# A two-layer hybrid diffusion backbone: first normalisation stage two tiles ahead, mean pools inside the pool projection, late row stores on ScalarE's queue

## The reference

```
ada = silu(cond) @ w_ada[l] + b_ada[l]            # 6 rows of 1024 per layer: shift, scale, gate, twice
u   = layer_norm(x) * (1 + sc1) + sh1
proj = u @ w_in_even                               # q 512 | k 128 | v 128 | p 512
pool = (mean of p over a window of 2, 4, 8 or 16 tokens) - p, per group of 128 channels
attn = attention(rms_norm(q), rms_norm(k), v)
x = layer_norm(alpha * x + g1 * (concat(attn, mix(pool)) @ w_out))
```

## Time and profile before

| | us |
|---|---|
| median of three executions | 2863.35 |
| the profiled execution | 2858.01 |
| its span | 2856.4 |
| first stage, until the last tile is in `act_a` | 0 to 122 |
| pool projection with the late half-blocks | 122 to 205 |
| q, k, v projection | 209 to 312 |

### The profile page before, as it was taken

The page is one execution under the profiler, slowest core; times in us unless marked ns, Lnnn a source line. Parts: engine busy times, 40 slices in busy tenths (PEclk is TensorE's granted clock), DMA queues, the critical chain, the costliest instruction groups (busy, mean ns, idle before and its releaser), DMA issues.

```text
span 2856.4 us, 36166 instructions
## 1 busy us (share of the span) xinstructions
PE 2682.8 (94%) x13884; PEld 2381.2 (83%) x13884; DVE 1537.1 (54%) x2157; ACT 921.3 (32%) x1402; POOL 432.5 (15%) x258
## 2 busy tenths in 40 slices
PE   5698799999899999999998799999899999999997
PEld 2477577768899999999997799978899999999996
DVE  1316588866555555555557433346555555555557
ACT  2521377745422222222124521125422222222223
POOL 1125277734000000000005200014000000000002
PEclk7899899999999999999999899999999999999999
DMA  9770100022311111111111212122311111111112
GB/s 335 270 262 7 60 1 0 1 90 74 133 45 44 44 44 37 44 30 44 37 45 67 74 45 74 56 92 79 128 45 44 44 44 42 39 39 35 38 35 81
DMA packets 171521, 196.08 MB, mean 69 GB/s; under 512 B 7628, under 2 KB 125880, under 8 KB 171442
## 3 DMA queue, kind: packets, MB, share of 16 engines
q1 hardware_dynamic: 169748, 194.33, 20.6%
q0 software_dynamic: 1280, 0.33, 0.1%
q10 hardware_dynamic: 411, 0.34, 0.0%
HBM read 175.64 MB, written 19.33 MB: 68 GB/s over the span
## 4 chain that ended last, share of the span: by engine, by line
PE 81%; DVE 7%; ACT 5%; POOL 3%; issue 2%; DMA 2%; SPq 0%; ACTq 0%; POOLq 0%; DVEq 0%
PE ps L2011 47%; PE ps L2231 18%; PE ps L1978 5%; POOL p_low L814 2%; PE ps L1961 1%; DVE small L1538 1%; ACT ln_u L939 1%; DVE stats L1391 1%; PE ps L2063 1%; PE ps L2164 1%; ACT p_exp L1068 1%; ACT p_top L870 1%; DMA ada_w<-in_w_ada 1%; PE ps L1923 1%; PE ps L2121 1%
## 5 line engine op out<-in xcount | busy, mean ns | idle before, releaser
L2011 PE MATMUL ps<-act_b,uw 128*128 128x384 f32 x4608 | 807.2, 337 | 7.9 <-DVE act_b L1357 6.5
L2011 PEld LDWEIGHTS ps<-act_b,uw 128*128 128x128 f32 x4608 | 803.5, 189 | 9.8 <-DVE act_b L1357 7.0
L2011 PEld LDWEIGHTS ps<-act_a,uw 128*128 128x128 f32 x3456 | 606.7, 190 | 17.5 <-issue 9.2
L2011 PE MATMUL ps<-act_a,uw 128*128 128x384 f32 x3456 | 613.2, 339 | 6.8 <-DVE act_a L1357 5.3
L2231 PE MATMUL ps<-dw,hh 128*128 128x512 f32 x2112 | 503.8, 398 | 9.0 <-DVE acc L1651 8.8
L2231 PEld LDWEIGHTS ps<-dw,hh 128*128 128x128 f32 x2112 | 398.7, 189 | 109.1 <-DVE acc L1651 10.2
L1651 DVE TENSOR_TENSOR acc<-acc,ps 128x512 f32<-128x512 f32 x360 | 246.0, 687 | 216.0 <-PE ps L2231 216.0
L870 ACT ACTIVATE fa<-ps 128x384 f32<-128x384 f32 (+2 forms) x176 | 67.3, 410 | 838.7 <-PE ps L2011 838.7
L1357 DVE TENSOR_TENSOR uw<-raw_u,uw 128x1024 fp32r<-128x1024 f32 x112 | 136.6, 1221 | 120.6 <-ACT uw L870 117.3
L1612 DVE TENSOR_SCALAR ft<-fa,fgrp 128x1153 f32<-128x1153 f32 x44 | 38.8, 881 | 298.9 <-ACT fa L870 284.1
L814 POOL TENSOR_TENSOR p_low<-p_exp,p_top 128x1536 fp32r<-128x1536 f32 (+1 forms) x50 | 170.6, 3412 | 94.8 <-ACT p_top L870 94.8
(11 more groups left out here) (208 smaller groups left out, 3127.2 us busy)
## 6 DMA issues: line engine op xcount, KB each, us to landing
raw_u<-in_w_up SPq DMA_DIRECT2D x88, 512.0 KB, 4.0
ada_w<-in_w_ada SPq DMA_DIRECT2D x52, 512.0 KB, 6.8
late_w<-in_w_ada SPq DMA_DIRECT2D x44, 512.0 KB, 6.3
raw_d<-in_w_down SPq DMA_DIRECT2D x44, 512.0 KB, 3.7
raw_u<-in_w_in_odd SPq DMA_DIRECT2D x20, 512.0 KB, 3.9
ln_y<-in_x_all SPq DMA_DIRECT2D x18, 512.0 KB, 5.4
xs<-ln_y SPq DMA_DIRECT2D x18, 512.0 KB, 2.6
acc<-xs SPq DMA_DIRECT2D x6, 1536.0 KB, 12.0
```

Of the source, the lines that this page charges most:

```text
L2011: mm = pe.matmul(out, uw[:, u_slot, w, k, :], src[:, k, a, c * CH:(c + 1) * CH], start=(k, w, a) == (0, 0, 0), stop=(k, w, a) == (KD - 1, ...
```

## The change

Cut to its core; what is left out renames or repeats.

```diff
 def ada_half(m):                     # other columns for m = 4 to 13, same set
 def ada_steps(kind):
-    return {s: [4 + s] for s in range(9)} if kind == "in" else {}
+    return {s: [s + 2] for s in range(2, 11)} if kind == "in" else {}
-        ada_row = at("ada_row", [P, 3, 512], F32, off_s + 28672)
+        ada_row = at("ada_row", [P, 6, 512], F32, off_s + 24576)
+        ada_side = at("ada_side", [P, 3, 512], F32, off_s + 12288)
# SP
-                        sp.wait_ge(z_rdy, NT)
+                        sp.wait_ge(zt_done, NT)
-            for m in range(3):
-                ada_units(m)
+            ada_units(0)
+            ada_units(1)
+            first_x(0)
+            ada_units(2)
+            ada_units(3)
+            first_x(1)
+            first_x(2)
+            ada_units(4)
             for n in range(2):
                 u_unit(n, u_source(n))
-            ada_units(3)
-            for s in range(3):
-                sp.dma_start(ln_y[:, s, :], dram_rows(t["x_all"], s)).then_inc(x_ld[s], 16)
-            ada_units(4)
-                            sp.wait_ge(z_rdy, tile + (NT * i4 + 1))
+                            sp.wait_ge(zt_done if i1 is None else z_rdy, tile + (NT * i4 + 1))
-                        for m in ada_steps(kind).get(3 + j, []):
-                            ada_units(m, i)
+                        if i1 is None:
+                            ada_units(5 + j, i)
-            for n in range(2, 4):
-                u_unit(n, u_source(n))
-            for k in range(2):
-                d_unit(D_QKV + k, t["w_in_even"][0][k * P:(k + 1) * P, 0:AW], AW)
             ln_loads("in", t["x_all"])
+            ada_units(11)
+            u_unit(2, u_source(2))
+            u_unit(3, u_source(3))
+            wq_unit(0)
+            wq_unit(1)
+            ada_units(12)
# GpSimd
-            for m in range(ADA_TOP, ADA_ALL):
+            for m in range(ADA_TOP, ADA_LATE):
...
-            gp.wait_ge(bank_free[0], 3 + 6)
-            gp.wait_ge(bank_free[1], 3 + 6)
-            gp.wait_ge(brow_mm, 6)
-            for a in range(2):
-                o = gp.memset(vv[:, :, a, 1, :].bitcast(F32), 1.0 - a)
-            o.then_inc(v_one, 1)
+            gp.wait_ge(u_split, 2 + U_FFN0)
             for g, w in enumerate(WINDOWS):
+                gp.wait_ge(bank_free[g % 2], 3 * (g // 2 + 2))
+                if g == NPG - 1:
+                    gp.wait_ge(brow_mm, 6)
+                    for a in range(2):
+                        o = gp.memset(vv[:, :, a, 1, :].bitcast(F32), 1.0 - a)
+                    o.then_inc(v_one, 1)
# ScalarE
             def late_evac(m):
                 copy(late_row[e % 2][:], ps[:, 6 + m % 2, :]).then_inc(ada_bank, 1)
+                act.wait_ge(ada_bank, m + 4)
+                for c in range(2):
+                    act.dma_start(ada[l, c::2, half * 512:half * 512 + 512], late_row[e % 2][c::32, :]).then_inc(late_st[e % 2], 16)
-            for m in range(ADA_TOP):
+            for m in range(2):
                 top_evac(m)
-            for n in range(2):
-                u_hi_at(n, 0, n)
+            def first_norm(s):
+                if s.live(2):
+                    tile = s.tile(2)
+                    if s.first(2):
+                        act.wait_ge(cols_done, 2)
+                    act.wait_ge(zt_done, tile + 1)
+                    if not s.first(2):
+                        act.wait_ge(act_rdy, tile)
+                    for k in range(KD):
+                        o = act.activation(ln_u[:, k * P:(k + 1) * P], ps[:, 6 + k // 4, (k % 4) * P:(k % 4 + 1) * P], ACT.Identity, ...)
+                    o.then_inc(mod_done, 1)
+                st, y = stats[:, s.slot(0), :], ln_y[:, s.slot(0), :]
+                if s.live(0):
+                    act.wait_ge(stat2, s.tile(0) + 1)
+                    act.activation(st[:, 34:35], st[:, 33:34], ACT.Sqrt, bias=eps, scale=1.0).then_inc(sd2, 1)
+                if s.live(2):
+                    copy(act_a[:, :, 0, bass.ds(tile * P, P)], ln_u[:]...).then_inc(act_hi, 1)
+                if s.live(0):
+                    act.wait_ge(rs2, s.tile(0) + 1)
+                    act.activation(y, y, ACT.Identity, bias=st[:, 36:37], scale=st[:, 35:36]).then_inc(z_rdy, 1)
+                if s.i is None and s.base == 0:
+                    top_evac(2)
+                    top_evac(3)
+                elif s.i is None and s.base == 1:
+                    for n in range(2):
+                        u_hi_at(n, 0, n)
-            act.wait_ge(ada_used, ADA_SLOTS + 4 * ADA_LATE)
+            act.wait_ge(ada_bank, 3 + ADA_LATE)
# VectorE
+            def first_norm(s):
+                if s.live(0):
+                    v.wait_ge(x_ld[s.slot(0)], s.third(0) * 16 + 16)
+                    norm_stats(ln_y[:, s.slot(0), :], st, 20).then_inc(stat2, 1)
+                    v.wait_ge(sd2, tile + 1)
+                    norm_scale(st, 20).then_inc(rs2, 1)
+                for m in ada_steps("in").get(s.base, []):
+                    ada_evac(m, s.i)
+                if s.live(2):
+                    v.wait_ge(act_hi, tile + 1)
+                    lo(act_a[:, :, 1, bass.ds(tile * P, P)], ln_u[:]..., act_a[:, :, 0, bass.ds(tile * P, P)]).then_inc(act_rdy, 1)
+                if s.i is None and s.base < 2:
+                    cols_of(range(s.base, s.base + 1))
+                    if s.base:
+                        u_lo_at(0, 0, 0)
+                        u_lo_at(1, 0, 1)
# TensorE
-            for m in range(ADA_TOP):
-                ada_block(m)
-            top_cols()
+            for n in range(2):
+                ada_block(2 * n)
+                ada_block(2 * n + 1)
+                top_cols(n)
+            pe.wait_ge(cols_done, 2)
             def ln_turn(tile, i4):
+                z = ln_z if i4 else ln_y[:, tile % 3, :]
-                for s in range(NT + 1):
-                    for m in ada_steps(kind).get(s, []):
-                        ada_block(m)
-                    if s == 6:
-                        next_chunk(0)
-                    if s:
-                        ln_turn(s - 1, LN[kind]["i4"])
-                    if s == NT:
-                        next_chunk(1)
+                for tile in range(NT):
+                    if tile == 5:
+                        next_chunk(0)
+                    ln_turn(tile, 0)
+                    ada_block(ADA_TOP + tile)
+                next_chunk(1)
```

More of the change, by code:

```diff
@@ L525, in load @@
                     sp.dma_start(ln_y[:, slot, :], dram_rows(src, tile)).then_inc(x_ld[slot], 16)
-                for s in range(1, 3):
-                    for m in ada_steps(kind).get(s, []):
-                        ada_units(m)
                 def step(tile, slot, used):
@@ L894, in late_evac @@
             def late_evac(m):
+                l, half = ada_half(m)
                 e = m - ADA_LATE
@@ L958, in rounding @@
                             copy(dest[:, :, 0, bass.ds(tile * P, P)], ln_u[:].rearrange("p (k t) -> p k t", k=KD)).then_inc(act_hi, 1)
-                    if i1 is not None:
-                        rounding()
+                    rounding()
                     if i4 is not None and s.live(1):
@@ L968, in step @@
                         act.activation(ln_z[:], ln_y[:, s.slot(1), :], ACT.Identity, bias=st[:, 36:37], scale=st[:, 35:36]).then_inc(z_rdy, 1)
-                    if i1 is None:
-                        rounding()
-                if i1 is not None:
-                    for k in (1, 2, 3, 4):
-                        gate(k)
-                ln_steps(act, step)
-            ln_act("in", act_a)
+                for k in (1, 2, 3, 4):
+                    gate(k)
+                ln_steps(act, step)
+            def first_norm(s):
+                if s.live(2):
+                    tile = s.tile(2)
+                    cc = 1 if s.first(2) else 0
+                    if s.first(2):
[4 more added lines that the diff above has]
+                    for k in range(KD):
+                        o = act.activation(ln_u[:, k * P:(k + 1) * P], ps[:, 6 + k // 4, (k % 4) * P:(k % 4 + 1) * P],
+                                           ACT.Identity, bias=cols[:, 0, 0, k, cc:cc + 1], scale=cols[:, 0, 1, k, cc:cc + 1])
+                    o.then_inc(mod_done, 1)
[4 more added lines that the diff above has]
+                if s.live(2):
+                    tile = s.tile(2)
+                    act.wait_ge(mod_done, tile + 1)
+                    copy(act_a[:, :, 0, bass.ds(tile * P, P)], ln_u[:].rearrange("p (k t) -> p k t", k=KD)).then_inc(act_hi, 1)
+                if s.live(0):
[7 more added lines that the diff above has]
+                        u_hi_at(n, 0, n)
+            ln_steps(act, first_norm)
             def wkv_hi(k):
@@ L1401, in ada_evac @@
             def ada_evac(m, i=None):
-                slot, turn, used = (m - ADA_TOP) % 3, (m - ADA_TOP) // 3, ADA_SLOTS + 4 * m + 4
+                used = ADA_SLOTS + 4 * m + 4
```

(9 more changed lines are left out.)

59 lines of the change are left out of this document (27 added, 32 removed).

## The result

| | before | after |
|---|---|---|
| median, runs side by side | 2863.05 us (2859.19 to 2865.09, 5 runs) | 2846.34 us (2843.37 to 2849.38, 5 runs) |
| ratio to before, 95% interval | | 0.9944 (0.9931 to 0.9957) |
| the profiled execution, its span | 2858.01, 2856.4 us | 2847.15, 2845.5 us |

The forecast was 2845 us in 2836 to 2857. The gain by the medians is 16.7 us of the 18.1 that the sum gave; by the two profiled executions it is only 10.9 us. That difference matters further down.

The account below looks back on a forecast made before the run. Two holes ahead of 302 us were taken to bound it: SP's wait at 107 to 122 us and VectorE beside POOL at 226 to 266. -9.0 - 10.2 + 1.1 = -18.1 us gave 2839.9 profiled, 2845 us median, range 2836 to 2857.

Parts of the forecast that it names:

- The sum: Whole kernel: -9.0 for the release, -10.2 for the keys, +1.1 for the pools' new place, -18.1 us together.
- SP's release: End of the first stage: SP's long wait ends at 113.1 instead of 122.1 us, 9.0 us earlier.
- from there to the first of the seven key turns: Projection: pools and ScalarE's store issues delay a subtraction, the wkv loads and half-block 22; 1.1 us more, bounds 0 and 3.
- seven key turns: Transposes of the keys, undisturbed by POOL: 9.0 us each, 63.0 in place of 73.2, 10.2 us less.
- I take 3 us for both together: First stage: two DMA pauses, near 43 and 50 us, each between zero and 6.8 us, cost 3 us in all.
- Taking 5.0 us for the store to land: End of the first stage: POOL's second store lands in 5.0 us and ends SP's wait at 113.1 us.
- is late by up to 2.2 us: Projection: the one subtraction on the path, ahead of the wkv loads, waits for one POOL instruction, up to 2.2 us.
- Half of the loads are paced by slots anyway: Projection: a reason for taking only 1.1 us, within 0 and 3, for the late subtraction and its loads.
- The last step: From profile to median: the profiled execution lies 5.3 us under the median, so 2839.9 us becomes 2845 us.
- The exclusion moved with the pools: Rival, projection: six subtractions wait 2.2 us each, 13.2 us on the path; gain only 6.0, 2857 us; chance 0.08.
- The first stage did give its time: Against the rival that the first stage gives nothing, pauses or the store's landing eating the head start: 2854 us; chance 0.17.
- The round trip: Rival, first stage: transposes, issue, landing and block follow each other, 12.5 us a turn for 7.25; 2884 us; chance 0.05.

Follow-up runs that it names:

- first stage alone: Changed kernel with mean pools and late stores back in their old place, only the new first stage kept; 2852.11 us, ratio 0.9970 to the kernel before.
- half-block 12 first: Changed kernel with the loads of half-block 12 ahead of four weight loads (u2, u3, wq 0 and 1) in SP's order; 2842.44 us, ratio 0.9928.
- all three edits: Changed kernel with chunk (0,0) behind the last tile's transposes, half-block 22 ahead of the wkv loads, half-block 12 ahead of four weight loads; 2835.86 us, ratio 0.9911.
- chunk last: Changed kernel with chunk (0,0) of the column sums moved from ahead of tile 5's transposes to behind the last tile's; by itself 2840.82 us, ratio 0.9924.
- pools held back: Changed kernel with POOL's third group of mean pools waiting until the last wq subtraction is made on VectorE; 2843.02 us, ratio 0.9932.
- pools alone: Kernel before with only the new place of pools and late stores, its first stage as it was; 2855.72 us, ratio 0.9976.

## Why the prediction was right, and where it was wrong

The sum, term by term, in the three profiles of the changed kernel against the first of before (122.14, 228.83 and 302.06 us):

| us | predicted | measured |
|---|---|---|
| SP's release | -9.0 (-13 to 0) | -7.0, -8.7, -4.6 |
| from there to the first of the seven key turns | +1.1 (0 to 3) | +7.9, +5.7, +6.7 |
| seven key turns | -10.2 (-11 to -7.5) | -10.9, -10.9, -10.9 |
| sum | -18.1 | -10.0, -13.9, -8.8 |

The second row is the shift of the transpose at 228.83 less that of the release: +0.9, -3.0 and +2.1, less the row above. Against the second profile of before (123.23, 228.58 and 302.03 us) the release gains 1.1 us more, the second row loses 1.3 more, and the turns gain 0.2 more.

**The keys: right.** Seven turns took 62.3 us (292.05 - 229.76), 8.9 each, where 63.0 were forecast and 73.2 stood before. Off by 0.7 us, because the undisturbed turns are a little under 9.0. The 128x128 multiply is at 284 ns with POOL silent. POOL's first pool came at 156.6 us (155 forecast), and the fourth group was through at 225.2, ahead of the rotation, as the step said.

**The release: right in kind, the pauses mis-sized.** The store decides, as forecast: the low part was written at 112.48 us (111.26 + 1.22) and the release came at 115.16. The modulations were 7.1 us apart (45.52 to 102.16 us, eight turns; 7 forecast). The step that failed is "I take 3 us for both together", and the places of the pauses with it: the stretch from 45 to 107 us has a share of 0.95 where it was 1.02, which over 62 us is 4.3 us. No pause came at 43 us: the columns were ready at 38.0 us (37.83 + 0.17) and not at 41.4, SP issued the rows of tile 3 at 40.23 us, and from 41 to 45 us the share is 1.11. The one at about 50 us came (0.35 of 6 us, 2.1), and another stood at 78 to 84 us, also about 2.1, which I had not looked for. In the old order the chunk stood ahead of the same transposes, but SP waited for `ln_z` and not for the transposes, and the share at 78 to 84 us was 1.00; in the new order the next loads waited for the chunk. Half-block 12's last load was therefore used at 108.66 us and not at 104.4. Taking 5.0 us for the store to land gave back half: it took 2.4.

**The pools' new place: the mechanism named, the size wrong by a factor of five to seven.** The step said of one subtraction on the path that it "is late by up to 2.2 us", that the ScalarE issue adds about 1, and then "Half of the loads are paced by slots anyway"; it took 1.1. The place was right: subtraction, `wkv` loads, half-block 22. ScalarE's part was sized right: its two issues took 1.00 us and moved the pair by 1.2. POOL's part was not: a pair of subtractions met it, not one, and took 4.30 us for 1.29, so that half-block 22 was issued 4.74 us behind the start of the pair (183.23 - 178.49) where it was 1.74 before (186.41 - 184.67). And half of the loads are paced by slots in the kernel before, as said, but no longer once the delay outlasts the slots: then it reaches all four loads. TensorE's waits at half-block 22 grew from 1.6 us to 4.6, 2.6 and 5.9 in the three profiles. The 5.7 to 7.9 us of the table hold these waits and the clock that follows; with the first stage alone the same row is -0.9 (220.14 and 114.33 us).

By the Trainium skill ("SBUF — State Buffer", Who interferes with whom) the port pair that VectorE and GpSimd share is held as an exclusive lock. The pairs of 1.29 us (POOL quiet) and 4.30 or 4.87 us (POOL beside) agree with it.

**And then the clock, which the forecast did not price.**
```profile
195.00:209.00 14.00, 13.28 (x73) 11.51 (x74) 1.52 (x5) 2.72 (x5) 0.03 (x1) 0.74 0.38 126
```

```profile
195.00:209.00 14.00, 13.28 (x82) 11.40 (x75) 2.26 (x5) 1.63 (x3) 9.11 (x13) 0.88 0.09 26
```

From the chunk behind half-block 22 to the first product took 13.99, 13.94 and 13.96 us in the three profiles of the changed kernel and 10.67 with the first stage alone: 3.3 us more for the same work. Set against that run, the first profile loses 9.6 us by the first key turn (229.76 less 220.14): 0.6 lay there before, 4.8 arose at half-block 22 (3.5 of longer waits, 1.3 of slower products), 3.3 are the clock up to the first product, and 0.9 lie behind it.

**Why the median still fell on the forecast.** The sum was too large by 4 to 9 us. The last step took the profiled execution to lie 5.3 us under the median and added that. It was so for the kernel before (2858.0 and 2858.6 profiled, medians of 2861.4 to 2863.1), but not for the changed kernel (2847.2 profiled and a median of 2846.3; 2852.9 and 2849.3). For a profiled execution the forecast was 2839.9; 2847.2, 2845.3 and 2852.9 were measured, so that number alone would have been too low. Two errors cancelled, by luck: the median is no proof of the sum. Why the profiled executions of before lie under their median stays open: executions without a profile have no stages to compare. Stages that the change doesn't touch scatter too: the third profile lost 2.8 us of its lead over before between 1586 and 1912 us.

Of the rivals, none took place as told. The exclusion moved with the pools, as the third said, but through one pair of subtractions and the clock, not through six waits. The first stage did give its time, to the point where the pools took it. The round trip did not come.

**Not tried:** the pause at 48 to 54 us, which stays in every version with the new first stage (share 0.59 to 0.67), and taking ScalarE's part of the lateness away by itself.

## What to carry to other kernels

A hole that is filled from two sides is best split before it is believed: each half was run alone, and only that showed that one gave 8.8 us and the other took them back at its seam. When an engine's work moves beside another's, find each instruction there that releases a load, price it at the disturbed duration and as often as it occurs, ask whether the slots that paced those loads still do so when it is late, and add what TensorE loses in clock behind the wait; often it is cheaper to reorder the queue so that nothing urgent stands behind the disturbed instruction than to remove the disturbance. And after moving loads earlier, look again at what TensorE does ahead of the instruction that releases the next load.

## What the runs showed of the hardware

- A small store's landing depends on what is in flight. From the end of its issue to SP's release it took 2.3 to 2.5 us in the three profiles of the changed kernel; in the first of them the loads were running out just then (DMA share 1.05 at 108 to 112 us, 0.22 at 112 to 116). It took 4.9 us with half-block 12 first, issued into full traffic (1.16 at 104 to 108, 1.03 at 108 to 112), 4.8 with all three edits, and 3.0 to 3.6 in the other three profiles with the chunk last. The Trainium skill ("DMA: Bandwidth & Descriptors", Latency and other measured facts) says that the fixed cost is smaller under a lighter load on memory; these numbers agree in direction. Whether memory or the engines' queues cause it, the runs don't tell.
- What a short wait of TensorE costs behind it comes in two sizes, and the length of the wait doesn't choose between them. From the chunk behind half-block 22 to the first product stands the same work in all of these runs. It took 10.7 to 11.4 us behind waits of 1.1 us (first stage alone), 2.1 (pools held back), 4.2 (chunk last) and 4.6 (pools alone), and 13.9 to 14.0 behind 2.6, 4.6 and 5.9 (the changed kernel) and 4.2 (half-block 12 first). The wait is what TensorE did before its clock fell in the second group; what decides whether it falls, the runs don't show. So of the changed kernel's loss the wait follows from the loads, while the 3.3 us of clock can be there or not.
